# One offset for both layers' operands, weight lower halves 128 bytes further on, and products in pairs

## The reference, cut to what matters

```
h = rmsnorm(x);  z = h @ w_in                        # 1024 -> 7168
A = (u * (tril(w_s) @ rmsnorm(gelu(v)) + b_s)) @ w_a
B = (b * conv3(c * xin)) @ w_b
x += (sigmoid(ga) * A + sigmoid(gb) * B) @ w_o
h = rmsnorm(x);  q = h @ w_q                         # 1024 -> 2048
e, g = top 16 of 16384 experts per head, softmax     # 8 heads, product keys
x += sum over e of  g * gelu(h . u_tab[e]) * v_tab[e]
x += sigmoid(rmsnorm(x) @ w_pg) * (p @ w_ple)
```

## Time and profile before

| | |
|---|---|
| median of three runs | 2256.3 us (2255.12 to 2257.0) |
| the profiled execution | 2254.77 us |
| its span, first to last instruction | 2253.1 us |
| TensorE matmuls | 15792, engine busy 2231.6 us (99%) |
| TensorE weight loads | 15792, 2088.5 us (93%), beside the matmuls |
| DVE, ACT, POOL busy | 1706.2, 1353.1, 854.6 us |
| mean granted TensorE clock | 0.999 |

### The profile page before, as it was taken

One profiled execution on the slowest core, in us unless ns is written; L12 is line 12 of the kernel. 1 busy time (PEld: TensorE's weight loads), 2 busy tenths in 40 slices (PEclk: granted clock), 3 DMA queues, 4 the chain that ended last, 5 costly groups with the idle time before them and its releaser, 6 DMA issues.

```text
span 2253.1 us, 49289 instructions
## 1 busy us (share of the span) xinstructions
PE 2231.6 (99%) x15792; PEld 2088.5 (93%) x15792; DVE 1706.2 (76%) x3283; ACT 1353.1 (60%) x2705; POOL 854.6 (38%) x766
## 2 busy tenths in 40 slices
PE   8999999999999999999999999999999999999998
PEld 8999999999999888888999999999999998888887
DVE  6556769966888788788874567699488878878887
ACT  6544546667777555555764545566677775555555
POOL 3100108988777122121121001299877761111110
PEclk9999999999999999999999999999999999999999
DMA  6545455555444899888554455455554458888884
GB/s 222 162 142 168 167 175 167 186 180 185 158 158 157 267 309 324 268 306 287 170 192 159 144 168 184 140 186 186 186 172 156 157 181 276 299 306 270 291 273 137
DMA packets 127141, 462.94 MB, mean 205 GB/s; under 512 B 14704, under 2 KB 14864, under 8 KB 126288
## 3 DMA queue, kind: packets, MB, share of 16 engines
q1 hardware_dynamic: 106416, 385.20, 49.1%
q0 software_dynamic: 20640, 76.68, 12.0%
HBM read 457.87 MB, written 3.95 MB: 205 GB/s over the span
## 4 chain that ended last, share of the span: by engine, by line
PE 97%; DVE 2%; issue 1%; ACT 0%; POOLq 0%; POOL 0%; DVEq 0%; ACTq 0%
PE ps L1435 21%; PE ps L1440 20%; PE ps L1436 20%; PE ps L1673 10%; PE ps L1674 10%; PE ps L1675 10%; PE ps L1629 1%; PE ps L1630 1%; PE ps L1588 1%; PE ps L1551 0%; POOLq L323 0%; DVE w_lo L874 0%; DVE h_lo L913 0%; PE ps L1553 0%; PE ps L1534 0%
## 5 line engine op out<-in xcount | busy, mean ns | idle before, releaser
L397 POOL TENSOR_TENSOR w_lo<-raw,w_hi 128x512 fp32r<-128x512 f32 x508 | 645.0, 1292 | 256.6 <-ACT w_hi L498 159.2
L1435 PE MATMUL ps<-h_hi,w_hi 128*128 128x256 f32 (+1 forms) x2592 | 653.9, 289 | 10.2 <-DVE h_lo L855 8.0
L1436 PE MATMUL ps<-h_lo,w_hi 128*128 128x256 f32 (+1 forms) x2592 | 641.7, 283 | 0.0
L1435 PEld LDWEIGHTS ps<-h_hi,w_hi 128*128 128x128 f32 x2592 | 489.4, 189 | 11.6 <-issue 9.5
L1436 PEld LDWEIGHTS ps<-h_lo,w_hi 128*128 128x128 f32 x2592 | 489.8, 189 | 0.2
L476 ACT ACTIVATE w_hi<-raw 128x1024 fp32r<-128x1024 f32 x334 | 351.6, 1053 | 190.6 <-PE ps L1440 189.7
L1243 DVE TENSOR_TENSOR w_lo<-raw,w_hi 128x512 fp32r<-128x512 f32 x504 | 347.7, 690 | 126.5 <-ACT w_hi L724 85.2
L1674 PE MATMUL ps<-w_lo,h_hi 128*128 128x512 f32 x1016 | 398.5, 392 | 0.0
L1675 PE MATMUL ps<-w_hi,h_lo 128*128 128x512 f32 x1016 | 398.5, 392 | 0.0
L1673 PE MATMUL ps<-w_hi,h_hi 128*128 128x512 f32 x1016 | 398.5, 392 | 0.0
L874 DVE TENSOR_TENSOR w_lo<-raw,w_hi 128x1024 fp32r<-128x1024 f32 x208 | 256.5, 1233 | 186.6 <-ACT w_hi L476 185.5
(11 more groups left out here) (225 smaller groups left out, 2971.0 us busy)
## 6 DMA issues: line engine op xcount, KB each, us to landing
raw<-stream SPq DMA_DIRECT2D x730, 512.0 KB, 3.4
bias<-bias_in POOLq DMA_DIRECT2D x2, 1152.0 KB, 6.8
x_keep<-x POOLq DMA_DIRECT2D x2, 1152.0 KB, 5.3
x<-x_keep POOLq DMA_DIRECT2D x2, 1152.0 KB, 9.6
x<-x_in SPq DMA_DIRECT2D x4, 288.0 KB, 5.3
y_out<-t_op SPq DMA_DIRECT2D x4, 288.0 KB, 2.1
ws<-ws_in POOLq DMA_DIRECT2D x2, 512.0 KB, 4.2
ring<-u_rows,rows POOLq DMA_INDIRECT x44, 5.9
```

Of the source, the lines that this page charges most:

```text
L397: return pool.tensor_tensor(w_lo[:, k % 2, lo_col:hi_col], raw[:, k, lo_col:hi_col], w_hi[:, k % 2, lo_col:hi_col].bitcast(F32), ALU.subtract)
L1435: pe.matmul(out, wh, rhs_hi, start=first, stop=False)
L1436: pe.matmul(out, wh, rhs_lo, start=False, stop=False)
```

## The change

Four edits are made, and no instruction is added or removed. (1) The lists of moving operands have no 32 bytes more in layer 1: both layers use layer 0's places. (2) 128 bytes that nobody uses are put ahead of `w_lo` and 128 behind it, so `w_lo` starts 128 bytes further on in the 512-byte grid than `w_hi`, and `h_hi`, `h_lo` and all that lies behind them 256 bytes further on. (3) In the u_tab stage the eight products with `w_lo` run over the chunks in the order 0, 2, 1, 3, 4, 6, 5, 7 instead of 0 to 7. (4) In the v_tab stage the three products of tile 0 run as upper*`w_hi`, lower*`w_hi`, upper*`w_lo`, and those of tile 1 as upper*`w_lo`, upper*`w_hi`, lower*`w_hi`.

```diff
+PAIRED = [0, 2, 1, 3, 4, 6, 5, 7]
...
         w_hi = sb("w_hi", [P, 2, D], F32R)
+        sb("ahead_of_w_lo", [P, 32], F32)
         w_lo = sb("w_lo", [P, 2, D], F32R)
+        sb("behind_w_lo", [P, 32], F32)
         h_hi = sb("h_hi", [P, C, T], F32R)
...
-        prompt_hi = [spaced(h_hi, 0, 288, C), spaced(h_hi, 8, 288, C)]
-        prompt_lo = [spaced(h_lo, 0, 288, C), spaced(h_lo, 8, 288, C)]
-        mixed_hi = [spaced(h_hi, 0, 256, 4), spaced(h_hi, 8, 256, 4)]
-        mixed_lo = [spaced(h_lo, 0, 256, 4), spaced(h_lo, 8, 256, 4)]
+        prompt_hi = [spaced(h_hi, 0, 288, C), spaced(h_hi, 0, 288, C)]
+        prompt_lo = [spaced(h_lo, 0, 288, C), spaced(h_lo, 0, 288, C)]
+        mixed_hi = [spaced(h_hi, 0, 256, 4), spaced(h_hi, 0, 256, 4)]
+        mixed_lo = [spaced(h_lo, 0, 256, 4), spaced(h_lo, 0, 256, 4)]
...
-                            for c in range(C // 2):
+                            for c in PAIRED[0:C // 2]:
                                 m = with_lower(out, j, c * P, prompt_hi[L][c], False)
...
-                            for c in range(C // 2, C):
+                            for c in PAIRED[C // 2:C]:
...
-                            m = with_lower(out, j, c * P, prompt_hi[L][c], c == C - 1)
+                            m = with_lower(out, j, PAIRED[c] * P, prompt_hi[L][PAIRED[c]], c == C - 1)
...
-                            pe.matmul(out, m_up, wh, start=first, stop=False)
-                            pe.matmul(out, m_up, wl, start=False, stop=False)
-                            m = pe.matmul(out, m_low, wh, start=False, stop=last)
+                            three = [(m_up, wh), (m_low, wh), (m_up, wl)]
+                            if tile:
+                                three = [three[2], three[0], three[1]]
+                            pe.matmul(out, three[0][0], three[0][1], start=first, stop=False)
+                            pe.matmul(out, three[1][0], three[1][1], start=False, stop=False)
+                            m = pe.matmul(out, three[2][0], three[2][1], start=False, stop=last)
```

## The result

The changed kernel takes 2260.05 us (median of 20 runs, 2257.79 to 2262.2) against 2255.06 us before (20 runs beside it, 2254.47 to 2257.0): ratio 1.0022, 95% interval 1.0016 to 1.0029. It is 0.2% slower, where 22 us less were forecast. The profiled execution has a span of 2258.1 us, 5.0 more than before.

A forecast was written before the change was run, and what follows sets the result against it. TensorE's distance between product starts, set by operand places, was taken to bound the kernel. -10.24 - 1.71 - 3.41 - 6.83 = -22.2 us takes the profiled 2254.8 to 2232.6; runs lie 1.5 higher: 2234 us, range 2228 to 2245.

The forecast's parts named there:

- the term of -6.83 us: v_tab, both layers: new order and `w_lo` 128 bytes on cut a unit from 2720 to 2693.3 ns, times 256 units.
- a trip from a to b for two products and back saves 13.3 ns: v_tab: a is an operand at the weights' place within 256 bytes, b 128 bytes off; one trip saved per six products.
- no gain: v_tab: lower bound of the saving from order and shifted `w_lo`, 0 us; the other bound was -10.24 us.
- The pair term, -3.41 us,: u_tab: reordered chunks pair the eight `w_lo` products, each falling from 118.3 to 116.7 ns, 13.3 ns a unit, 256 units.
- the same cycle entered elsewhere: u_tab: with `w_lo` moved 128 bytes and `h` 256, its eight products run b b a a instead of a a b b.
- One offset, -10.24 and -1.71 us,: Layer 1 at layer 0's places gets layer 0's product distances: -10.24 us in v_tab, -1.71 us in u_tab.
- The projections: Products of 288 columns: the eight with `w_lo` swap places; 0 us taken, 4.2 us either way at most.
- The other engines' cover: DVE, POOL and transfers stay hidden behind TensorE; POOL keeps 216 ns spare in a 2800 ns u_tab unit.
- places do nothing: Rival: operand places don't matter and layer 1 is slower for another reason; 2256 us, chance 0.04.
- The offset alone counts: Rival: pairs and the shift give nothing in v_tab; 2244 us, 2241 to 2247 with the projections' bounds, chance 0.22.
- b is cheap by itself: Rival: all products 10.0 ns or less above their columns, the projections' lower products gaining too; 2226 us, chance 0.10.
- The 512-byte pattern: Rival: places repeat every 512 bytes, not 256, so both v_tab stages take 2.80 us a unit; 2261 us, chance 0.04.

The follow-up runs named there:

- e11: Changed kernel without the pads, v_tab products cut in two of 256 columns (all but a layer's first and last unit): 2279.63 us, single run.
- e12: Changed kernel with both pads, v_tab products cut in two of 256 columns (all but a layer's first and last unit): 2277.65 us, single run.
- e2: Kernel before plus only the two 128-byte pads around `w_lo`: 2268.21 us, ratio 1.0058.
- e6: Kernel before without layer 1's 32 bytes, with 128 bytes ahead of `w_lo` and 384 behind, so only `w_lo` changes its place in the grid: 2267.17 us.
- e9: Changed kernel without the pad ahead of `w_lo`, 128 bytes behind it, so activations stand 128 bytes off both weights: 2263.46 us.
- e10: Changed kernel without the pad ahead of `w_lo`, 64 bytes behind it, so activations stand 64 bytes off: 2266.19 us.
- e7: Changed kernel without the two pads, its other three edits kept: 2239.73 us, ratio 0.9931.
- e1: Kernel before with only layer 1's extra 32 bytes removed, so both layers use layer 0's places: 2243.15 us, ratio 0.9947.
- e8: Changed kernel with 384 instead of 128 bytes behind `w_lo`, so `h` keeps its old place in the grid: 2259.07 us.
- e5: Kernel before without layer 1's 32 bytes, with 256 bytes behind `w_lo`, so activations move 256 bytes and the weights stay: 2243.05 us.

## Why the prediction was wrong

**The step that failed** is the term of -6.83 us, "a trip from a to b for two products and back saves 13.3 ns". It was measured on products of 256 columns and carried to products of 512, with "no gain" as its worst bound. With 512 columns the trip costs: six products took 2760 / 2 = 1380 ns in layer 0 instead of 1360, where 1346.7 were forecast. In place of -6.83 us the term measured +5.1 us in layer 0 and +6.8 us in layer 1 (353.4 and 355.1 against 348.3). e11 and e12 show that the length of the stream decides the sign. The reason given for carrying it, that the extra above the columns is of one size at both lengths, compared equal places at 512 columns with pairs at 256. For equal places it holds: e11's 2880 / 24 = 120.0 ns are 13.3 above 106.7, as at 512. For pairs it doesn't: 10.0 ns at 256 columns in the u_tab stage, 1380 / 6 - 213.3 = 16.7 ns here. And the bounds left out a loss, though the slow layer, 2.80 us a unit, stood there as the price of a place off the weights: e2, e6, e9 and e10 all meet just that price, 358.5 us a stage.

**The pair term, -3.41 us,** was right by itself and wrong beside the pad. Without pads the u_tab stages fall by 1.6 us through edit 3 (e7 against e1, in both layers) where 1.7 was forecast. The step that failed is "the same cycle entered elsewhere": with `w_lo` 128 bytes on, the products with `w_lo` and those with `w_hi` stand in opposite phase at both borders of a unit, and the 16 with `w_hi`, which were to stay, take 1.88 to 1.89 us in the changed kernel. That is +4.0 us in each layer (e8 against e7), and +1.8 us with the old order of chunks (e6 against e1). Where the cycle is entered elsewhere but `w_lo` and `w_hi` stay in step (e9), a u_tab stage takes 395.1 us where about 394 had been expected, 1.1 more than in e7, so most of the 4.0 comes from the two being out of step.

**One offset, -10.24 and -1.71 us,** was right within 0.1 us, and so was the mechanism: e1 measures -10.2 and -1.6. In the changed kernel it drowned: the pads raise a v_tab stage from 348.3 to 353.4 us or more. The sum as measured: -11.9 for the offset and -3.4 for pairs in both layers (e7 against e1), then +20.3 for the pads (2260.05 - 2239.73), which makes the +5.0. Of the 20.3, 11.9 lie in the v_tab stages and 8.1 in the u_tab stages.

**The other terms.** The projections moved by 0.3 us (0, at most 4.2). The other engines' cover held: no new wait stands in TensorE's list.

**The rivals.** That places do nothing falls with e1; the Trainium skill's rule of independent read ports (page "SBUF — State Buffer", section "Who interferes with whom") does not describe these products, whose distance is 226.7 or 233.3 ns by the address alone. "The offset alone counts" is e1's result but not the changed kernel's. "b is cheap by itself" falls with e9, where all products are b and dear. The 512-byte pattern, the one rival on the slower side, falls with e5: it was `w_lo`'s 128 bytes that cost and not `h`'s 256. That its 2261 us lie so near the measured 2260 is luck: it had v_tab stages of 2.80 us a unit, where 2.76 and 2.78 were measured, and a gain of 5.1 us in the u_tab stages, which lost 3.2. The range ended at 2245 because that case was left out of it at 0.04, and because no case held the plain one: that products with `w_lo` pay the slow layer's price, as they do with the old order in e2 and e6.

**What stays open** is why the length decides. A lag between the stream and the weight load that a longer product works off and a shorter one hands to the next would fit, but no run shows the lag itself.

## What to carry to other kernels

Before operands are moved to spare a conflict, take the price of the new place from products of the same length: a saving seen at 256 columns was a loss at 512. For 512 columns the cheap case here was moving and stationary operands that start at the same place modulo 256 bytes, in every product; every other case tried cost 6.7 ns more a product or, with the products with `w_lo` in pairs, 3.3 to 4.4. And a bundle of edits is best timed part by part: three of these four together gave 0.9931, and the fourth took all of it back.

## What the runs showed of the hardware that was not expected

- In the v_tab stage each of the three starts off the weights' place that were run, by 32 bytes (before, layer 1), 64 (e10) or 128 (e9), costs the same 2.80 us a unit, not a price that grows with the distance; and lone products off it (e6, one in three) make all three as dear.
- The same products at the same places and in the same order settled into two rhythms in one execution: 353.4 us in layer 0 and 355.1 us in layer 1 of the changed kernel, while e8 has 353.4 in both. The changed kernel's runs also spread over 4.4 us, those of before over 2.5. No run tells what sets the rhythm.
